# Where the first weight chunk is issued: from third place on SP's queue to first place on ScalarE's

## The reference

```python
mem_n = rms_norm(mem, norm_mem_g)
h = rms_norm(x, norm_in_g[layer])
proj = jnp.einsum('bsd,de->bse', h, w_in[layer])
...
mkv = jnp.einsum('bmd,de->bme', mem_n, w_mem_kv[layer])
mk, mv = jnp.split(mkv, 2, axis=-1)
```

## Time and profile before

| | us |
|---|---|
| three runs of the kernel before | 2172.07, 2172.87, 2173.11 |
| the profiled execution, its own time | 2173.86 |
| span of the profiled execution, first to last instruction | 2172.1 |
| around the span (own time less span) | 1.8 |
| TensorE busy | 2160.1 (99%) |
| ScalarE busy | 1072.1 (49%) |
| VectorE busy | 1375.4 (63%) |
| mean granted TensorE clock | 0.999 of full |

### The profile page before, as it was taken

One profiled execution on the slowest core, in us unless ns is written; L12 is line 12 of the kernel. 1 busy time (PEld: TensorE's weight loads), 2 busy tenths in 40 slices (PEclk: granted clock), 3 DMA queues, 4 the chain that ended last, 5 costly groups with the idle time before them and its releaser, 6 DMA issues.

```text
span 2172.1 us, 25610 instructions
## 1 busy us (share of the span) xinstructions
PE 2160.1 (99%) x9642; PEld 1793.4 (83%) x9642; DVE 1375.4 (63%) x1764; ACT 1072.1 (49%) x1358; POOL 169.3 (8%) x285
## 2 busy tenths in 40 slices
PE   9999999999999999999999999999999999999998
PEld 7888888888888888888888888888888888888887
DVE  5866777776576654646777888665555555554444
ACT  5745555554455444444645666354444444444443
POOL 0011101111000000000111101120000000000000
PEclk9999999999999999999999999999999999999999
DMA  8777667768755757678878756697777777776664
GB/s 302 219 232 228 207 183 226 221 201 258 226 159 156 231 185 220 206 237 267 253 262 259 223 184 198 211 275 215 212 215 228 212 212 216 224 237 193 194 192 154
DMA packets 231412, 474.13 MB, mean 218 GB/s; under 512 B 17032, under 2 KB 17296, under 8 KB 230416
## 3 DMA queue, kind: packets, MB, share of 16 engines
q1 hardware_dynamic: 212128, 409.00, 61.1%
q0 software_dynamic: 18736, 62.93, 9.6%
q10 hardware_dynamic: 448, 0.86, 0.1%
HBM read 442.31 MB, written 30.41 MB: 218 GB/s over the span
## 4 chain that ended last, share of the span: by engine, by line
PE 96%; DMA 1%; DVE 1%; ACT 0%; issue 0%; POOL 0%; SPq 0%; DVEq 0%; ACTq 0%
PE ps L1652 31%; PE ps L1648 31%; PE ps L1647 31%; PE ps L1560 1%; PE ps L1576 1%; DMA stage<-bounce 1%; DMA bounce<-tmp 0%; DMA raw<-in_w_mem_kv 0%; PE ps L1529 0%; DVE w_lo L958 0%; ACT w_hi L624 0%; PE ps L1683 0%; PE ps L1681 0%; PE ps L1682 0%; DVE tmp L1138 0%
## 5 line engine op out<-in xcount | busy, mean ns | idle before, releaser
L958 DVE TENSOR_TENSOR w_lo<-raw,w_hi 128x1024 fp32r<-128x1024 f32 (+1 forms) x776 | 932.4, 1210 | 707.2 <-ACT w_hi L624 705.1
L624 ACT ACTIVATE w_hi<-raw 128x1024 fp32r<-128x1024 f32 (+1 forms) x776 | 811.9, 1050 | 902.5 <-PE ps L1652 815.1
L1647 PE MATMUL ps<-w_hi,xT_hi 128*128 128x512 f32 x1088 | 427.3, 393 | 0.0
L1648 PE MATMUL ps<-w_hi,xT_lo 128*128 128x512 f32 x1088 | 424.2, 390 | 0.0
L1652 PE MATMUL ps<-w_lo,xT_hi 128*128 128x512 f32 x1088 | 291.1, 390 | 0.2 <-DVE w_lo L958 0.2
L1648 PE MATMUL ps<-w_hi,u2T_lo 128*128 128x512 f32 x704 | 274.4, 390 | 0.0
L1647 PE MATMUL ps<-w_hi,u2T_hi 128*128 128x512 f32 x704 | 274.2, 389 | 0.0
L1652 PEld LDWEIGHTS ps<-w_lo,xT_hi 128*128 128x128 f32 x1088 | 204.3, 188 | 43.1 <-DVE w_lo L958 0.7
L1648 PEld LDWEIGHTS ps<-w_hi,xT_lo 128*128 128x128 f32 x1088 | 204.5, 188 | 42.1
L1647 PEld LDWEIGHTS ps<-w_hi,xT_hi 128*128 128x128 f32 x1088 | 204.3, 188 | 42.2
L1652 PE MATMUL ps<-w_lo,u2T_hi 128*128 128x512 f32 x704 | 188.3, 390 | 0.0
(11 more groups left out here) (266 smaller groups left out, 2283.1 us busy)
## 6 DMA issues: line engine op xcount, KB each, us to landing
raw<-in_w_in SPq DMA_DIRECT2D x368, 512.0 KB, 4.5
raw<-in_w_ffn_gate SPq DMA_DIRECT2D x88, 512.0 KB, 4.2
raw<-in_w_ffn_up SPq DMA_DIRECT2D x88, 512.0 KB, 4.5
raw<-in_w_ffn_down SPq DMA_DIRECT2D x88, 512.0 KB, 4.8
raw<-in_w_out SPq DMA_DIRECT2D x64, 512.0 KB, 5.5
bounce<-tmp POOLq DMA_DIRECT2D x50, 512.0 KB, 3.3
stage<-bounce POOLq DMA_DIRECT2D x160, 128.0 KB, 5.1
raw<-in_w_mem_kv SPq DMA_DIRECT2D x32, 512.0 KB, 6.1
```

Of the source, the lines that this page charges most:

```text
L624: nc.scalar.activation(w_hi[:, s, 0:per], raw[:, s, 0:per], ACT.Copy).then_inc(hi_ready, 1)
L958: nc.vector.tensor_tensor(w_lo[:, s, 0:per], raw[:, s, 0:per], w_hi[:, s, 0:per].bitcast(F32), ALU.subtract)\
L1647: nc.tensor.matmul(acc, part(hi, k, t), w_hi[:, s, k], start=h == 0 and k == 0, stop=False)
L1648: nc.tensor.matmul(acc, part(lo, k, t), w_hi[:, s, k], start=False, stop=False)
```

## The change

The load of the first chunk (rows 0 to 255, columns 0 to 511 of `w_mem_kv`, into `raw` slot 0, semaphore `raw_in[0]`) is taken out of SP's list and put in front of the two vector loads on ScalarE's queue. SP's list is walked as before, with the callback `load_mem(1)` in its place; only the DMA of chunk 0 and its wait are left out. The amount of data is the same.

```diff
--- before.py
+++ after.py
@@ -483,13 +483,17 @@
         def _(sp):
             w = Walk()
 
-            def load(tile, then={}):
+            def load(tile, then={}, skip=()):
                 per = tile.get("per", 2)
                 src = tile["w"].rearrange("(c p) n -> p c n", p=P)
                 if w.loop:
                     sp.to_reg(tile["col"] * 4)
                 for h in chunks(tile):
                     s = w.n["g"] % SLOTS
+                    if h in skip:
+                        w.step("g")
+                        then[h]()
+                        continue
                     sp.wait_ge(lo_ready, w("g", 1))
                     sp.dma_start(raw[:, s, 0:per], src[:, h * per:(h + 1) * per, bass.ds(tile["col"], NW)])\
                       .then_inc(raw_in[s], 16)
@@ -512,7 +516,7 @@
             sp.dma_start(ident, consts_d[:, C_ID:C_ID + P]).then_inc(in_const, 16)
             load_mem(0)
             first, second, *rest = tiles_memkv()
-            load(first, {0: lambda: load_mem(1), 2: lambda: load_mem(2), 3: lambda: load_mem(3)})
+            load(first, {0: lambda: load_mem(1), 2: lambda: load_mem(2), 3: lambda: load_mem(3)}, skip=(0,))
             load(second, {h: lambda h=h: load_x(h // QUAD, h % QUAD) for h in range(NT * QUAD)})
             sp.dma_start(consts[:, C_ID + P:], consts_d[:, C_ID + P:]).then_inc(in_tables, 16)
             load_all(rest + tiles_attention() + tiles_merge(0))
@@ -850,6 +854,7 @@
             four[3]["act_hooks"][5] = [log_sigmoid_exp]
             for h, a, b in ((0, 0, 3), (1, 3, 6), (2, 6, 9), (4, 9, 12), (5, 12, 13), (7, 13, 16)):
                 four[3]["act_hooks"].setdefault(h, []).append(lambda a=a, b=b: move_x(3, a, b))
+            act.dma_start(raw[:, 0, 0:2], w_mkv.rearrange("(c p) n -> p c n", p=P)[:, 0:2, 0:NW]).then_inc(raw_in[0], 16)
             act.dma_start(vec_a[:, :], vecs[0:P]).then_inc(in_vec, 16)
             act.dma_start(vec_b[0:V_END - P, :], vecs[P:V_END]).then_inc(in_vec, 16)
             act.wait_ge(pool_c, 1)
```

## The result

The kernel after takes 2175.91 us (median of 20 runs, 2175.35 to 2177.67); the kernel before takes 2172.8 (median of 20, 2172.07 to 2177.46). The ratio is 1.0013, 95% interval 1.0007 to 1.0019: about 3 us slower, which is under the 0.2% that was called no change, but clear of zero. The profiled execution took 2175.35 us, with a span of 2173.5.

The account below looks back on a forecast made before the run. TensorE bounds it, gapless from its first product. Vectors at 6.3 plus 5.35 put L1710 at 11.65, 1.83 us later than 9.82; 2173.86 becomes 2175.7, from the median 2174.7 us; range 2171.8 to 2177.0.

Parts of the forecast that it names:

- a shift of L1710 reaches the end: TensorE's first product, started at 9.82 us: no gap follows, so any delay there delays the end by as much.
- The vectors' landing, T = 6.3: Start of TensorE's first instruction, which waits for the vectors: from 3.37 to 6.3 us, by even sharing between two queues.
- the first rival: Vectors on ScalarE's queue not held by the chunk: landing at 3.9 us, -0.6 us, 2172.3, at best 2171.8; chance 9%.
- From T to the first product, 5.35 us: Distance from TensorE's first instruction to L1710: measured distances kept, less the wait for the chunk, 8.72 - 3.37 = 5.35 us.
- The chunk's own wait: ScalarE's wait for the first chunk before the first `w_hi`: taken as gone, at most -1.10 us.
- No gain to take at all: In an undisturbed run the chunk may land before 7.52 us anyway: loss 2.9 us, 2175.8; chance 15%.
- What was booked at nothing: ScalarE's table load and activation 0.5 us later, memory quarter by about 6.9 us, SP's earlier issues: all hidden, worth nothing.
- The slower rival: L1735's wait: vectors behind a late chunk part; from 8.8 us the loss passes 0.2%, 9.2 gives 2177.6; chance 5%.
- The clock: TensorE's granted clock: full in every stretch from the start, idle transposes moving with the vectors, so nothing booked.
- Order in the queue: ScalarE's DMA queue: descriptors go in ring order, so vectors cannot land before the chunk is nearly through; a loss.

Follow-up runs that it names:

- the second profile of before: The kernel before, run again with no edit for a second profile: 2172.53 us, ratio 0.9996.
- first try for a faster kernel: Against the kernel before: ScalarE's queue issues the identity, the two vectors, then the chunk; SP's queue starts with the memory quarter. 2175.65 us, ratio 1.001.

## Why the prediction was right, and which term was off

- **What bounds the kernel, and that a shift of L1710 reaches the end.** Right. Against the second profile of before, F is 3.03 us later (11.77 - 8.74) and the span 2.8 (2173.5 - 2170.7), and TensorE is busy for all of the time from 12 to 2160 us in both; the 0.2 us between the two numbers stay unexplained. The 13 profiles together say it better. Take the instant at which the eight opening products end and the next transposes of the memory begin (11.74 in the first profile of before, 10.68 in the second, 13.79 with the change): the own time of the execution is 2161.5 to 2162.4 us more than this instant in twelve of them, and 2163.3 in the one with a wait of 0.9 us later on.
- **The vectors' landing, T = 6.3.** Near: 6.76 and 6.63. That the loads issued ahead of the vectors make them late is shown: T is 3.40 with the vectors first on the queue, 6.7 with one chunk ahead and 9.93 with two. The working of the size does not hold. It shared the engines evenly by bytes. At 5.2 us the chunk's queue had moved 0.54 MB and SP's 0.38; then SP's moved 0.54 MB while the last 127 packets of the vectors, 0.05 MB, went through; and by 6.7 us 1.51 MB had moved, not 1182 KB. By packets the two queues were nearly level at 5.2 us (305 and 296), and a packet of the vectors holds about 0.4 KB on average, one of the chunk about 1.9 KB. Sharing that goes more by packets than by bytes would explain why the small load comes so late, but no run tests that. The other thing missed is what a large load on the other queue does alone: with the vectors free of the chunk on their own queue, T was still 5.15 (vectors on SP's queue) and 6.49 (first try for a faster kernel), where the first rival had 3.9. These two differ so much that the runs do not say how the 3.4 us divide into place in the queue and sharing.
- **From T to the first product, 5.35 us.** It was 5.01 in both profiles. That L1715 started at 11.77 and 11.64 where 11.65 was forecast is therefore in part luck: T was 0.3 to 0.5 us too early and this distance 0.34 too long. The transposes of the memory followed T by 1.92 and not 2.07, because the quarter had landed meanwhile; and `w_hi` starts 0.11 us before `memT_hi` ends (10.57 against 9.84 + 0.84), where 7.52 assumed 0.02 us behind its end.
- **The chunk's own wait, "at most -1.10 us", taken in full.** This is the term that was mis-sized. It was read from one execution in which the chunk landed late; in the second profile there is no such wait, and the change gives nothing there. The step that went wrong is in the sum: the shift was counted from 9.82, in an execution with the wait, and then added to a median that was 1.0 us lower. That excess is the size of the wait, so the wait was very likely missing from the median already. The sum without it is the case "No gain to take at all": 2.9 us, 2175.8, against 2175.91 measured, with the same luck in it. It was given 15%.
- **What was booked at nothing.** The later table load and small activation are hidden (ScalarE idle for 5.96 us ahead of `memT_hi`, up from 3.34), and the memory quarter is hidden, landed at 1.2 + 5.6 = 6.8 where 6.9 was named as the latest. TensorE shows no wait that SP's earlier issues could have shortened.
- **The slower rival** (a late part behind which the vectors stand, T over 8.8) was not seen in the three profiles with this queue order: 6.63, 6.76 and, with the idle transposes moved, 7.09.
- **The clock.** It was booked at nothing and is nearly that: in the first profile of the change the six idle transposes ahead of the first product took 1.49 us instead of 0.82 and the first product 0.57 instead of 0.47, which is 0.1 us; in the second they took 0.87 and 0.47. But the reason given, a granted clock that is full from the start, did not carry it. That column reads 1.00 also where the products stand 0.43 us apart. With the vectors on SP's queue this cost 1.0 us, and in the first try for a faster kernel, where the eight products took 2.61 us, 0.7.
- **Order in the queue.** The rows show it: 127 of the vectors' packets after 5.2 us, and T = 9.93 with two chunks ahead. The Trainium skill, page "DMA: Bandwidth & Descriptors", section "Queues, rings and completion order", has the rule that on each DMA engine a queue's descriptors are taken in ring order, and the trace agrees in kind. The chunk's issue did move 0.93 us ahead (1.68 to 0.75), but the chunk was not what TensorE waited for.

## What to carry to other kernels

At the start of a program, order loads by when they are needed, the small ones that everything waits for ahead, and let no large load be issued ahead of them on another queue either: what was saved for one load was taken from another in every order tried here. Before booking a wait as a gain, compare the profiled execution's own time with the median of the other runs; an excess of the size of the wait is a strong hint that the median does not have it, and a second profile settles it. And an idle stretch that a reordering opens ahead of TensorE's first products can cost as much through the clock as through the delay: with the vectors ahead of the chunk, 1.6 us beside the 1.7 by which F was late (10.40 against 8.74).

## What the runs showed of the hardware

- 68 KB of vectors were there by 3.3 to 3.4 us when the first large load was issued some 0.45 us behind the first of them, and only by 5.15 to 6.49 us when it was issued 0.45 us ahead of them on the other queue. Issued at the same time as the large load, their last packet moved at 4.3 to 4.5 us and not at 2.6 to 2.7. Why so small a lead matters that much was not tested further.
- Two queues at work together did not move equal bytes. With the change, ScalarE's and SP's queue moved 0.54 and 0.38 MB by 5.2 us (305 and 296 packets) and 0.05 and 0.54 MB from there to 6.7 us (127 and 278 packets).
- POOL's first DMA, issued at 1.27 us, moved its first packet only after 5.5 us.
- With 2.39 us of idleness ahead of the first products the granted clock was 0.60 and 0.54 in the stretches from 10 to 12 and 12 to 14 us; with transposes up to 9.9 us it was 1.00. With 1.82 us of idleness it had not fallen: the products after it stood 0.23 us apart (10.12, 10.35, 10.59).
- At the start of an execution TensorE was slow under a granted clock that reads 1.00: six idle transposes took 1.54 us and later 0.82, and products stood 0.43 us apart until 13.17 us in the profile with the vectors on SP's queue.
